# The last output tile of a streaming-encoder block split 384 and 128 tokens in place of 256 and 256

## The reference, cut to what matters

```python
def rmsnorm(x, g):
    xf = x.astype(jnp.float32)
    y = xf * lax.rsqrt(jnp.mean(xf * xf, axis=-1, keepdims=True) + EPS)
    return (y * g.astype(jnp.float32)).astype(x.dtype)
...
        x = x + 0.5 * swiglu(rmsnorm(x, ffn2_norm[l]), ffn2_w_gu[l], ffn2_w_down[l])
    return rmsnorm(x, final_norm)
```

## Time and profile before

| | |
|---|---|
| median of 3 runs | 1118.38 us (1118.32 to 1120.45) |
| profiled execution, its own time | 1120.16 us |
| its span | 1118.2 us |
| TensorE busy | 1106.8 us, 99% |
| VectorE, ScalarE, GpSimd busy | 626.9, 522.2, 437.1 us |
| mean granted TensorE clock | 0.999 |
| DMA | 135.33 MB, mean 121 GB/s |

### The profile page before, as it was taken

The page is one execution under the profiler, slowest core; times in us unless marked ns, Lnnn a source line. Parts: engine busy times, 40 slices in busy tenths (PEclk is TensorE's granted clock), DMA queues, the critical chain, the costliest instruction groups (busy, mean ns, idle before and its releaser), DMA issues.

```text
span 1118.2 us, 17287 instructions
## 1 busy us (share of the span) xinstructions
PE 1106.8 (99%) x6358; PEld 971.0 (87%) x6358; DVE 626.9 (56%) x911; ACT 522.2 (47%) x725; POOL 437.1 (39%) x544
## 2 busy tenths in 40 slices
PE   9999999999999999999999999999999999999997
PEld 7889999988888888888888888888889999988886
DVE  6887777441222668888567123464787777440012
ACT  6545555542323555654466443354455555542221
POOL 0000000486665544434548883173000000485651
PEclk9999999999999999999999999999999999999999
DMA  7276775332323221222313442122187675332312
GB/s 240 76 210 188 194 197 169 114 112 96 113 94 111 77 76 57 76 76 76 113 57 133 163 157 76 39 81 102 45 226 188 178 197 169 114 113 96 112 57 76
DMA packets 48626, 135.33 MB, mean 121 GB/s; under 512 B 4672, under 2 KB 10944, under 8 KB 48448
## 3 DMA queue, kind: packets, MB, share of 16 engines
q1 hardware_dynamic: 43344, 118.38, 30.2%
q0 software_dynamic: 4032, 14.68, 7.7%
q10 hardware_dynamic: 1200, 1.57, 0.4%
HBM read 132.52 MB, written 2.10 MB: 120 GB/s over the span
## 4 chain that ended last, share of the span: by engine, by line
PE 53%; POOL 25%; issue 21%; DVE 0%; POOLq 0%; DMA 0%; ACT 0%; DVEq 0%; SPq 0%; ACTq 0%
POOL wl L438 25%; PE bank L1420 9%; PE bank L1422 9%; PE bank L1421 9%; PE bank L1522 4%; PE bank L1524 4%; PE bank L1523 4%; PE score L1523 3%; PE score L1522 3%; PE score L1524 3%; PE o_bank L1522 1%; PE o_bank L1524 1%; PE o_bank L1523 1%; PE bank L1479 1%; PE bank L1483 1%
## 5 line engine op out<-in xcount | busy, mean ns | idle before, releaser
L438 POOL TENSOR_TENSOR wl<-raw,wh 128x256 fp32r<-128x256 f32 x512 | 412.5, 839 | 326.0 <-ACT wh L472 281.8
L472 ACT ACTIVATE wh<-raw 128x1024 fp32r<-128x1024 f32 x124 | 130.1, 1054 | 162.2 <-PE bank L1422 158.1
L1420 PE MATMUL bank<-xh,wh 128*128 128x512 f32 x488 | 194.8, 399 | 0.0
L1422 PE MATMUL bank<-xh,wl 128*128 128x512 f32 x488 | 190.4, 390 | 0.0
L1421 PE MATMUL bank<-xl,wh 128*128 128x512 f32 x488 | 190.1, 390 | 0.0
L452 POOL DMA_DIRECT2D raw<-w_all x28 | 24.3, 869 | 330.1 <-DMA raw<-w_all 330.1
L1420 PE MATMUL bank<-zr,wh 128*128 128x512 f32 (+1 forms) x374 | 142.6, 381 | 0.0
L1422 PE MATMUL bank<-zr,wl 128*128 128x512 f32 (+1 forms) x374 | 141.7, 379 | 0.0
L1421 PE MATMUL bank<-zr,wh 128*128 128x512 f32 (+1 forms) x374 | 140.5, 376 | 0.0
L902 DVE SCALAR_TENSOR_TENSOR x<-bank,x 128x512 f32<-128x512 f32 (+1 forms) x31 | 21.3, 687 | 175.4 <-PE bank L1422 175.4
L1421 PEld LDWEIGHTS bank<-xl,wh 128*128 128x128 f32 x488 | 91.8, 188 | 19.9 <-issue 1.7
(11 more groups left out here) (304 smaller groups left out, 2493.8 us busy)
## 6 DMA issues: line engine op xcount, KB each, us to landing
raw<-w_all SPq DMA_DIRECT2D x200, 512.0 KB, 3.3
raw<-w_all POOLq DMA_DIRECT2D x28, 512.0 KB, 5.2
zf<-w_all SPq DMA_DIRECT2D x28, 256.0 KB, 4.5
x<-x_t SPq DMA_DIRECT2D x8, 256.0 KB, 6.2
out_t<-x SPq DMA_DIRECT2D x8, 256.0 KB, 2.4
raw<-w_all SPq DMA_DIRECT2D x6, 256.0 KB, 6.1
memf<-mem_t ACTq DMA_DIRECT2D x1, 1024.0 KB, 4.8
raw<-w_all ACTq DMA_DIRECT2D x2, 256.0 KB, 3.9
```

Of the source, the lines that this page charges most:

```text
L438: ins = nc.gpsimd.tensor_tensor(wl[:, slot, two], raw[:, slot, two], wh[:, slot, two].bitcast(f32), SUB)
L472: nc.scalar.activation(wh[:, slot, :], raw[:, slot, :], ACT.Copy).then_inc(hi_ready, 1)
L1420: nc.tensor.matmul(out_, a[0], b_[0], start=first, stop=False)
L1422: return nc.tensor.matmul(out_, a[1], b_[0], start=False, stop=last)
```

## The change

`HALVES` becomes 384 and 128 tokens. On VectorE the steps get two functions, `last_update(h)` and `scale_out(h, m)`, and another order: the update of part 1 now stands between the second and the third pair of part 0's scalings. The wait for the gains (`x_gain`) is made once. TensorE's, ScalarE's and SP's code is as it was; the widths of their instructions follow `HALVES`. The stores are the same eight, in the same order, with rows of 1536 bytes for part 0 and of 512 bytes for part 1.

```diff
-HALVES = [slice(0, T // 2), slice(T // 2, T)]
+HALVES = [slice(0, 3 * T // 4), slice(3 * T // 4, T)]
...
-            for h in range(2):
+            def last_update(h):
                 if h == 0:
                     dve.wait_ge(half_done, 1)
                 else:
                     dve.wait_ge(unit_used, NU)
                 xs = x[:, KC - 1, HALVES[h]]
                 V_.scalar_tensor_tensor(out=xs, in0=bank[(G_DOWN2 + KC - 1 + h) % 4][:, HALVES[h]], scalar=-0.5, in1=xs,
                                         op0=MULT, op1=ADD).then_inc(x_half, 1)
-                dve.wait_ge(rms_ready, R["final"] + h + 1)
-                dve.wait_ge(x_gain, KC - 1)
+
+            def scale_out(h, m):
+
                 inv = rstd[:, HALVES[h]]
-                for m in range(0, KC - 2, 2):
+                if m < KC - 2:
                     xs = x[:, m:m + 2, HALVES[h]]
-                    V_.tensor_tensor(xs, xs, inv.rearrange("p (a t) -> p a t", a=1).to_broadcast([128, 2, T // 2]), MULT)\
-                        .then_inc(out_new, 1)
-                xs = x[:, KC - 2, HALVES[h]]
-                V_.tensor_tensor(xs, xs, inv, MULT)
-                xs = x[:, KC - 1, HALVES[h]]
-                V_.scalar_tensor_tensor(out=xs, in0=xs, scalar=pcol("final", KC - 1), in1=inv,
-                                        op0=MULT, op1=MULT).then_inc(out_new, 1)
+                    both = inv.rearrange("p (a t) -> p a t", a=1).to_broadcast([128, 2, HALVES[h].stop - HALVES[h].start])
+                    V_.tensor_tensor(xs, xs, both, MULT).then_inc(out_new, 1)
+                else:
+                    xs = x[:, KC - 2, HALVES[h]]
+                    V_.tensor_tensor(xs, xs, inv, MULT)
+                    xs = x[:, KC - 1, HALVES[h]]
+                    V_.scalar_tensor_tensor(out=xs, in0=xs, scalar=pcol("final", KC - 1), in1=inv,
+                                            op0=MULT, op1=MULT).then_inc(out_new, 1)
+
+            last_update(0)
+            dve.wait_ge(rms_ready, R["final"] + 1)
+            dve.wait_ge(x_gain, KC - 1)
+            scale_out(0, 0)
+            scale_out(0, 2)
+            last_update(1)
+            scale_out(0, 4)
+            scale_out(0, 6)
+            dve.wait_ge(rms_ready, R["final"] + 2)
+            for m in range(0, KC, 2):
+                scale_out(1, m)
```

## The result

The changed kernel took 1121.60 us (median of 20 runs, 1120.59 to 1123.22) against 1119.35 (20 runs, 1118.20 to 1120.54). The ratio is 1.0022 with a 95% interval of 1.0015 to 1.0029, so it is slower by about 2.5 us, and by between 1.7 and 3.2 us at the ends of the interval. The prediction took 2.24 us as its line between no change and slower; the interval has that line inside it. The difference that was forecast was 2.3 us. The time that was forecast was 1120.7 us, and the measured one lies 0.9 us above it. The profiled execution has a span of 1120.3 us against 1118.2 and took 1122.25 us in all against 1120.16.

The account below looks back on a forecast made before the run. The prediction took TensorE, busy 99%, to bound the kernel, with only the tail touchable. TensorE's 3.65 us loss less 1.34 won back gave +2.3, added to the median 1118.38 for 1120.7 us; range 1118.2 to 1121.8.

Parts of the forecast that it names:

- First part 0.1733 per product, 11.44 us: TensorE, last tile: 66 products of 384 columns take 11.44 us in place of 7.77.
- Second part at the pace of loading, 0.111: TensorE, last tile: 66 products of 128 columns go at the weight-load pace, 7.33 us in place of 7.77; chance 0.78.
- by column: Rival on TensorE: second-part products pay by column, 0.062 each, end -0.9 us, 1117.5; chance 0.07.
- in between: Rival on TensorE: loads partly overlap products, 0.086 each in the second part, +0.7 us, 1119.1; chance 0.10.
- Sum 1.29: TensorE: the first part's sum over partitions, 384 wide, costs 1.29 us in place of 0.86, on TensorE's path.
- TensorE +3.65: TensorE's last product ends at 1113.41 against 1109.76, 3.65 us later.
- The line between 256 and 512 columns: TensorE: straight line through 0.1177 us at 256 and 0.2289 at 512 columns, giving 0.1733 at 384 and 0.062 at 128.
- Second update waits on VectorE, over 2 us: VectorE stands still from 1111.2 to 1113.61 for TensorE's last product, with two ready first-part steps queued behind.
- Root hidden by the steps behind the update (1.66 against 1.87): After the second update: second root ready 1.66 us later, while VectorE's remaining first-part steps take 1.87.
- Stores: Tail: large stores 1.04 us, small ones 0.43, moving back to back; 6.62 us from the update's end to the span's.
- dear small stores: Rival on the stores: a 512 B packet costs as much as a 1024 B one, +3.5 us, 1121.9; chance 0.05.
- Sum of the difference, +2.3: Whole span: 1120.51 against 1118.2, TensorE giving away 3.65 us and everything behind it winning back 1.34.

Follow-up runs that it names:

- e3: Against the changed kernel: split 272 and 240, second update back behind all first-part scalings; ratio to before 0.9996 (0.9987 to 1.0005).
- e4: Against the changed kernel: split 320 and 192, second update back behind all first-part scalings; ratio to before 1.0002 (0.9993 to 1.0011).
- e6: Against the changed kernel: split 448 and 64, old order of scalings; one profile, last tile to end 28.16 us against 24.85 before.
- e5: Changed kernel, second-part products using 64 of 128 weight columns, some outputs not computed; one profile, last tile to end 24.15 us against 24.85 before.
- e7: Changed kernel, second part loading high weights once for both data terms, 44 loads in place of 66, two updates; ratio to before 1.0003 (0.9994 to 1.0012).
- e1: Changed kernel with 384 and 128 kept, second update back behind all first-part scalings; ratio to before 1.0010 (1.0001 to 1.0019).
- e9: e1 with the second part's second and fourth store issued by ScalarE; one profile, last tile to end 26.25 us against 24.85 before.
- e8: Against the changed kernel: split 320 and 192, old order, high weights loaded once for both data terms; ratio to before 1.0003 (0.9994 to 1.0012).

## Where the prediction failed, and what it had right

The forecast time failed in its last term, the time of before to which the difference was added. The mechanism held, and the difference came out within 0.3 us.

- *First part 0.1733 per product, 11.44 us*: 11.44 measured.
- *Second part at the pace of loading, 0.111*: 0.112. The row of one-column matmuls, 0.112, held for fp32r loads as well; shown by e3, e4 and e6 (the width of the data makes no difference), e5 (the columns of the load do) and e7. The rivals "by column" (0.062) and "in between" (0.086) are out. The Trainium skill ("TensorE: Matmul & The Clock Gate", section "Back-to-back issue gap") gives about 81 ns for 128-column products; this trace does not agree, with 0.112. The same page of the Trainium skill, section "LDWEIGHTS (loading the stationary operand)", gives columns / 1.2 ns, an estimate of 107 ns for 128 columns; that is 5 ns below the 0.112 seen here.
- *Sum 1.29*: 1.29. *TensorE +3.65*: +3.64. The line between 256 and 512 columns held at 384, but not quite at 272 (e3) and 320 (e4), where it was 0.002 and 0.001 per product too low.
- *Second update waits on VectorE, over 2 us*: 2.31, with two steps behind it; ended by TensorE.
- *Root hidden by the steps behind the update (1.66 against 1.87)*: Exp was done 1.63 after the update's end at 1113.58, the scalings started 1.78 after it.
- *Stores*: small ones 0.45 (0.43 forecast) and large ones 1.10 (1.04), back to back; from the update's end to the end of the span 6.72 (6.62). The rival of dear small stores is out. The term that it left out is the issue. It put the issue of the last small store 3.47 after the update's end, right behind its scaling; it was issued at 1117.62, 4.04 after. At 0.4 to 0.7 us between issues small stores can be limited by SP's queue; in the changed kernel the large stores ahead of them hid that, in e1 they did not.
- *Sum of the difference, +2.3*: +2.41 from the last tile on, +2.25 between the medians, +2.5 by the ratio. The prediction gave 0.53 to slower and 0.44 to no change, by a line of 2.24 us. The interval of 1.7 to 3.2 us doesn't decide between the two, so the lean to slower is neither borne out nor refuted.
- *The step that failed* is the last: "I add the difference to the median: 1118.38 + 2.3 = 1120.7". The measured 1121.60 lies 0.9 higher, and all of that is the base: 1119.35 in place of 1118.38 is +0.97, and the difference of the medians is 0.05 below the 2.3. Of the three runs shown two were near 1118.3 and one at 1120.45. The prediction read this as scatter ("its three runs lie 2.13 us apart") and took the profiled execution's 1120.16 as lying above the median. The 20 runs show two groups, 1118.2 to 1118.8 and 1119.9 to 1120.5, ten in each, with nothing between. A median of three picks one of them, that of 20 (1119.35) falls in the gap. The changed kernel's 20 runs have two groups as well, 11 from 1120.6 to 1121.6 and 9 from 1122.2 to 1123.2, and their median, 1121.60, lies at the top of the lower one. So the two medians are not taken at the same place either: that their difference, 2.25, comes so near to 2.3 is in part luck. Group against group it is 2.6 and 2.3.

What the change bought: 1.23 us behind TensorE (8.44 to 7.21), where 2.05 were to be had with the old order. What it paid: 3.64 us of TensorE, of which 0.43 are the wider sum and 3.21 the loads, that is 66 products at 0.112 which would need some 0.062 to multiply (an estimate, by the line). 0.83 of the net loss is the order. The split and the order are not independent: at 256 and 256 the order is free.

## What to carry to other kernels

Before making products narrower, look for the pace of the narrowest ones in the trace. Here it was the pace of their weight loads, 0.112 us, and two parts of 66 products cost that floor on the narrow side and the full price of their columns on the wide one. When an instruction with a late release is moved ahead of others on the same engine, count what stands behind it and what their stores then stand in front of; it is free only while another wait covers it. When the runs of a kernel fall into groups, compare group with group, take the difference from the profile, and the base from more than three runs.

## What was not expected of the hardware

**Two groups of runs, 1.6 to 1.9 us apart, made in the first 11 us.** The group means are 1.9 us apart before and 1.6 in the changed kernel. The fourth group of four products starts at 10.35 in the profile of before and at 8.62 in that of e7, 1.73 apart; at the last tile the distance is 1.74 (1093.35 and 1091.61). After the first 16 matmuls, of a matrix of ones, TensorE waits 0.9 us for its first data. The first four products in the profile of before:

```profile
5.71 2.05 PE L1479 MATMUL bank<-xh,wh 128*128 128x512 f32 x4 [0.86 <-ACT xh L697]
```

and in the profile of e7:

```profile
5.79 1.16 PE L1505 MATMUL bank<-xh,wh 128*128 128x512 f32 x4 [0.93 <-ACT xh L698]
```

In the first, four products take 1.84 us from start to start of the next group (5.71 to 7.55), 0.46 each; in the second 1.00 (5.79 to 6.79), 0.25 each, and 0.23 in the groups behind. Only the profiles of e7 and e9 have the quick start, and their last tile begins at 1091.61 and 1091.85; in the other nine it begins at 1093.02 or later. 0.46 is twice 0.23, as it would be with a clock at the lower of its two levels, 1.2 in place of 2.4 GHz. The granted clock doesn't show that; in the profile of before it reads 1.00 in this microsecond (third value from the end):

```profile
6.00:7.00 1.00, 1.00 (x3) 0.81 (x3) 0.84 (x2) 1.00 (x3) 0.00 (x0) 1.00 1.05 350
```

So half the clock is argued from the factor of two, and not shown. The group of an execution does not hang on the kernel: both groups occur for before, changed and each of e1 to e4, e7 and e8, which is why E counts from the last tile. What decides between them stays open.

**Store issues on one queue stand 0.4 to 0.7 us apart** when the stores are ready sooner than that (e1: 1116.02, 1116.44, 1116.95, 1117.48; changed kernel: 1115.88, 1116.41, 1117.08, 1117.62), although one issue alone shows 0.37. Stores of 128 KB with 512 B rows move in 0.45 when the issues keep up.
